# Opening in two halves of the channels, with dummies on TensorE, a joined router and a shorter first gather, in a two-layer diffusion kernel

## What is computed

```python
for layer in range(DEPTH):
    last = layer == DEPTH - 1
    mod_l = (cond_lat @ w_mod[layer] + b_mod[layer])[:, None, :]
    sh1, sc1, gt1, sh2, sc2, gt2 = jnp.split(mod_l, 6, axis=-1)
    ...
    h_l = modulate(rmsnorm(x, g_norm1[layer]), sh1, sc1)
    out_l, out_c = token_mixer(h_l, h_c, w_in[layer], ...)
    x = x + gt1 * out_l
    h_l = modulate(rmsnorm(x, g_norm2[layer]), sh2, sc2)
    y = swiglu(h, ...) if layer % 2 == 0 else moe_swiglu(h, w_router, b_router, w1, w3, w2)
    x = x + gt2 * y
return rmsnorm(x, g_final)

def moe_swiglu(h, w_router, b_router, w1, w3, w2):
    logits = (h @ w_router).astype(jnp.float32) + b_router.astype(jnp.float32)
    top_v, top_i = lax.top_k(logits, TOP_K)
    top_w = jax.nn.softmax(top_v, axis=-1)
    combine = jnp.sum(jax.nn.one_hot(top_i, N_EXPERTS, dtype=jnp.float32) * top_w[..., None], axis=-2)
    for e in range(N_EXPERTS):
        out = out + combine[..., e:e + 1] * swiglu(h, w1[e], w3[e], w2[e])
```

## Time and profile before

| | us |
|---|---|
| median of 3 runs | 1991.55 (1990.99 to 1991.76) |
| profiled execution | 1990.3 |
| its span | 1988.5 |
| PE busy | 1925.8 |
| DVE busy | 1365.7 |
| ACT busy | 991.1 |

### The profile page before, as it was taken

One profiled execution on the slowest core, in us unless ns is written; L12 is line 12 of the kernel. 1 busy time (PEld: TensorE's weight loads), 2 busy tenths in 40 slices (PEclk: granted clock), 3 DMA queues, 4 the chain that ended last, 5 costly groups with the idle time before them and its releaser, 6 DMA issues.

```text
span 1988.5 us, 23322 instructions
## 1 busy us (share of the span) xinstructions
PE 1925.8 (97%) x9008; PEld 1532.1 (77%) x9008; DVE 1365.7 (69%) x1606; ACT 991.1 (50%) x1098; POOL 87.6 (4%) x127
## 2 busy tenths in 40 slices
PE   6999999999899999989999989999999999999997
PEld 3785666667688888868788978888888888888886
DVE  5752444477667646546354558989898988898995
ACT  3423333322522222244434367777777777777774
POOL 0150000010000001001200000000000000000000
PEclk9999999999899999989999979999999999999998
DMA  9322122255256556513234279999998999999980
GB/s 375 127 74 67 61 75 96 85 181 168 94 181 191 180 180 232 193 64 138 85 120 156 96 307 358 356 349 356 349 357 346 358 347 357 347 359 348 358 329 22
DMA packets 72398, 438.67 MB, mean 221 GB/s; under 512 B 9184, under 2 KB 9952, under 8 KB 28000
## 3 DMA queue, kind: packets, MB, share of 16 engines
q1 hardware_dynamic: 60624, 394.18, 52.9%
q0 software_dynamic: 11664, 43.00, 6.8%
HBM read 436.09 MB, written 1.05 MB: 220 GB/s over the span
## 4 chain that ended last, share of the span: by engine, by line
PE 90%; DVE 4%; ACT 3%; issue 1%; DMA 0%; SPq 0%; ACTq 0%; DVEq 0%
PE ps L1630 12%; PE ps L1631 12%; PE ps L1632 12%; PE ps L2020 8%; PE ps L2022 8%; PE ps L2021 7%; PE ps L1865 6%; PE ps L2034 4%; PE ps L2035 4%; PE ps L2038 4%; PE ps L1814 2%; PE ps L1773 2%; DVE elo L1443 1%; PE ps L1664 1%; PE ps L1840 1%
## 5 line engine op out<-in xcount | busy, mean ns | idle before, releaser
L1443 DVE TENSOR_TENSOR elo<-estage,ehi 128x2048 fp32r<-128x2048 f32 x264 | 604.8, 2291 | 74.4 <-ACT ehi L945 67.9
L945 ACT ACTIVATE ehi<-estage 128x2048 fp32r<-128x2048 f32 x264 | 505.4, 1914 | 53.9 <-PE ps L2038 50.4
L1630 PE MATMUL ps<-h_hi,whi 128*128 128x512 f32 (+1 forms) x960 | 369.6, 385 | 16.1 <-DVE h_lo L1098 8.8
L1631 PE MATMUL ps<-h_lo,whi 128*128 128x512 f32 (+1 forms) x960 | 346.8, 361 | 0.0
L1632 PE MATMUL ps<-h_hi,wlo 128*128 128x512 f32 (+1 forms) x960 | 346.6, 361 | 0.0
L2020 PE MATMUL ps<-ehi,xg_hi 128*128 128x512 f32 x704 | 283.9, 403 | 2.1 <-DVE xg_lo L1456 2.1
L2022 PE MATMUL ps<-ehi,xg_lo 128*128 128x512 f32 x704 | 276.3, 392 | 0.0
L2021 PE MATMUL ps<-elo,xg_hi 128*128 128x512 f32 x704 | 275.5, 391 | 0.0
L1058 DVE TENSOR_TENSOR wlo<-stage,whi 128x2048 fp32r<-128x2048 f32 x79 | 182.2, 2306 | 97.0 <-ACT whi L687 96.9
L687 ACT ACTIVATE whi<-stage 128x2048 fp32r<-128x2048 f32 x79 | 150.8, 1909 | 164.6 <-PE ps L1632 163.9
L1630 PEld LDWEIGHTS ps<-h_hi,whi 128*128 128x128 f32 x960 | 183.2, 191 | 57.9 <-issue 19.1
(11 more groups left out here) (224 smaller groups left out, 2331.7 us busy)
## 6 DMA issues: line engine op xcount, KB each, us to landing
estage<-in_moe SPq DMA_DIRECT2D x264, 1024.0 KB, 5.0
stage<-in_split SPq DMA_DIRECT2D x79, 1024.0 KB, 4.9
gw<-in_mods POOLq DMA_DIRECT2D x80, 512.0 KB, 4.0
dw<-in_direct SPq DMA_DIRECT2D x36, 512.0 KB, 3.7
mw_b<-in_mods SPq DMA_DIRECT2D x8, 512.0 KB, 12.7
mw_a<-in_early SPq DMA_DIRECT2D x8, 512.0 KB, 14.2
xT<-in_x SPq DMA_DIRECT2D x1, 2048.0 KB, 7.9
gw<-in_cond_rows SPq DMA_DIRECT2D x1, 1024.0 KB, 5.4
```

Source lines behind the costliest of these rows:

```text
L945: act.activation(ehi[:, w % SPLIT, :], estage[:, w % STAGE, :], ACT.Copy).then_inc(S("e_hi_done"), 1)
L1443: dve.tensor_tensor(elo[:, w % SPLIT, :], estage[:, w % STAGE, :], ehi[:, w % SPLIT, :], ALU.subtract)\
L1630: pe.matmul(out, hi, rhs_hi, start=first, stop=False)
L1631: pe.matmul(out, hi, rhs_lo, start=False, stop=False)
```

## The change

1. **Opening.** x is loaded in four DMAs ahead of everything but the condition; its squares go through DVE's adds, as in the other norms. The shifts and the scales (four groups of 512 columns) all come from PE: each group's 8 rows run in four column tiles of 32 columns (`cond_32`, the condition padded to 32 columns), and a matrix `pick` sums the four tiles while it turns them. Groups 0 and 1 hold shift and scale of channels 0 to 511, groups 2 and 3 of channels 512 to 1023; the norm's first half needs the first two. DVE's start units are gone, the `cond_rows` load and the work on it come behind the norm, and split unit 1 is placed inside the norm.
2. **Norms n1_0, n2_0, n1_1.** The second half (latent tokens) of odd k is scaled by DVE instead of ACT.
3. **Dummies.** `keep_clock` issues 128x128 matmuls whose result nobody reads: 16, 2 and 4 in the opening, 5, 4 and 12 around each later norm, 2 a channel in the router, 6 behind the first gather, 14 ahead of the last scatter.
4. **Out-projection of layer 0.** The last two `merged_lo` stand ahead of the last two modulation units.
5. **Routing.** Small DVE operations are joined over the two token tiles, both logits lie in one bank, the low rows are copied by DVE (ACT did), the first gather multiplies rows by selection the other way round and gives the turned tokens at once, waits are split in halves; exponential, combine and the turned selection move into the first expert.

```diff
@@ modulation rows and turns (PE)
         def early_rows(g):
             pe.wait_ge(S(f"early_in{g}"), 16 * GROUP_UNITS)
-            for k in range(KD):
-                u = GROUP_UNITS * g + k // 2
-                ins = pe.matmul(ps[2 + g][0:2, :], cond_t[:, k, :], mw_a[:, u, k % 2, :], start=(k == 0), stop=(k == KD - 1))
+            quarters = P // TILE_W
+            for i in range(KD // quarters):
+                for q in range(quarters):
+                    k = i * quarters + q
+                    u = GROUP_UNITS * g + k // 2
+                    w = (mw_a, mw_b)[u // (EARLY_UNITS // 2)][:, u % (EARLY_UNITS // 2), k % 2, :]
+                    ins = pe.matmul(ps[2 + g][TILE_W * q:TILE_W * (q + 1), :], cond_32[:, k, :], w, start=(i == 0), stop=(i == KD // quarters - 1))
@@ opening (PE)
-        first_squares()
+        def keep_clock(b, n):
+            for _ in range(n):
+                pe.matmul(ps[b][:, 0:P], ones[:, :], ident[:, :], start=True, stop=True)
+        keep_clock(0, 16)
+        added_squares("n1_0", 0)
+        keep_clock(0, 2)
         early_rows(0)
+        everywhere("n1_0", 0)
         early_rows(1)
         early_turn(0)
-        everywhere("n1_0", 0)
         early_turn(1)
+        early_rows(2)
+        keep_clock(0, 4)
@@ first tile of the in-projection, for each k (PE)
+                    if layer == 0 and j == 0 and k == KD // 4:
+                        early_rows(3)
+                    if layer == 0 and j == 0 and k == KD // 2:
+                        early_turn(2)
+                        early_turn(3)
@@ loads (SP)
+        for k in range(0, KD, 2):
+            sp.dma_start(xT[:, k:k + 2, :], A["x"][:, k:k + 2, :]).then_inc(S(f"x_in{k // 4}"), 16)
+        for u in range(EARLY_UNITS):
+            sp.dma_start(early(u), A["early"][u]).then_inc(S(f"early_in{u // GROUP_UNITS}"), 16)
+            if u == GROUP_UNITS - 1:
+                for t, a in small:
+                    load_small(t, a).then_inc(S("consts"), 16)
+            if u == 2 * GROUP_UNITS - 1:
+                load_split(0)
+        load_split(1)
+        sp.dma_start(gw[:, :, :], A["cond_rows"]).then_inc(S("cond_rows1"), 16)
@@ opening (DVE)
-        cond_rows(1)
-        mod_units("start", 0)
+        for k in range(1, KD - 1):
+            add_square("n1_0", 0, k)
         inverse_root("n1_0", 0)
-        mod_units("start", 1)
...
         split_lo(1)
-        mods(0, EARLY_MODS, FLUSH_TILES[0])
-        dve.wait_ge(S("mod_turned"), EARLY_GROUPS)
-        turned_mods()
-        dve.wait_ge(S("mods"), 4)
-        coefs(0, 0)
+        early_mods(0)
@@ norm (DVE)
+                if tag == "n1_0" and k == KD // 2:
+                    lo(k - 2)
+                    lo(k - 1)
+                    early_mods(1)
...
+                if tag == "n1_0" and k == KD - 2:
+                    split_lo(DENSE_SPLIT)
+                if shared(tag, k):
+                    second_half(k)
@@ norm (ACT)
+                if tag == "n1_0" and k == KD // 2:
+                    hi(k - 1)
+                    row_copies(2)
+                    act.wait_ge(S("norm_coef"), 2)
...
-                for s, at in parts:
+                for s, at in parts[:1] if shared(tag, k) else parts:
...
+                if tag == "n1_0" and k == KD // 2 + 1:
+                    split_hi(DENSE_SPLIT)
@@ merges of layer 0 (DVE)
                 merge(m)
+                if m == NM - 1:
+                    merged_lo(m - BESIDE - 1)
+                    merged_lo(m - BESIDE)
                 after_merge(m)
-                if m > BESIDE:
+                if BESIDE < m < NM - 1:
                     merged_lo(m - BESIDE - 1)
-            merged_lo(KD - 1)
@@ norms n2, n1_1 (PE)
+            keep_clock(7, 5)
             added_squares(f"n2_{layer}", lc)
+            keep_clock(7, 4)
             everywhere(f"n2_{layer}", lc)
+            keep_clock(7, 12)
@@ router (PE)
+            keep_clock(5, 2)
...
+            def first_gather():
+                pe.wait_ge(S("sel"), passed("sel", p) + 2)
+                for f in range(2):
+                    if p == 0 and f == 1:
+                        pe.wait_ge(S("most_ready"), 1)
+                    for n, rows in enumerate((htok_hi, htok_lo)):
+                        if p == 0:
+                            pe.wait_ge(S(("htok_hi", "htok_lo")[n]), 2 * (f + 1))
+                        for k in range(4):
+                            for t in range(2):
+                                ins = pe.matmul(ps[3 + 2 * n + f][:, k * SLOTS:(k + 1) * SLOTS], rows[:, t, (4 * f + k) * P:(4 * f + k + 1) * P], sel[:, t, :],
+                                                start=(t == 0), stop=(t == 1))
+                        ins.then_inc(S(("ga_full", "gt_full")[n]), 1)
...
-            gather(0, 0, 0)
-            gather(0, 0, 1)
+            first_gather()
+            if p == 0:
+                keep_clock(2, 6)
@@ first expert (DVE), tail (PE)
+                    if p == 0 and kind == "w" and cc == 2:
+                        combine()
+                        dve.sem_inc(S("comb"), 1)
...
+        keep_clock(2, 14)
         last_scatter("fn")
```

More of the change, by code:

```diff
@@ L191, in mod_plan @@
     return plan
-MOD_FLUSH = [("start", 1), ("in", 0, NT - 1), ("out", 0, KD - 2), ("upu", 4), ("down", 1, 3)]
+MOD_FLUSH = [("in", 0, NT - 1), ("out", 0, KD - 2), ("upu", 4), ("down", 1, 3)]
 def flush_units(n):
-    tiles = [("start", 0), ("start", 1)] + [key for key, _ in split_stream()]
+    tiles = [key for key, _ in split_stream()]
     upto = tiles.index(MOD_FLUSH[n])
@@ L478, in build @@
     junk = {
-        "start": Region(pool_in_at).take("junk_start", [P, D]),
         "in": Region(br_at + 2 * KB * T * 4).take("junk_in", [P, D]),
@@ L1189, in _ @@
             norm(f"n1_{layer}", 0)
+            if layer == 0:
+                cond_rows(1)
             for j, name in enumerate(TILES):
```

283 lines of the change are left out of this document (164 added, 119 removed).

## The result

| | us, median | runs |
|---|---|---|
| before | 1991.27 (1990.83 to 1991.76) | 4 |
| changed | 1972.41 (1971.67 to 1974.48) | 4 |

The ratio is 0.9908, 95% interval 0.9896 to 0.992: 18.9 us less, where the forecast's terms sum to 21.2. The profiled execution of the changed kernel took 1974.48, the longest of the four; its span is 1972.7, 15.8 less than before's. A second profile of the same kernel has a span of 1970.8 (17.7 less).

A forecast was written before the change was run, and what follows sets the result against it. TensorE (PE) was taken as the bound, busy 1925.8 of 1988.5 us, so only its waits and half clock could give time. Terms 7.0 + 4.4 + 1.0 + 6.5 (routing net) + 2.3 = 21.2 gave median 1970.3, range 1962 to 1982.

The forecast's parts named there:

- Opening, 7.0: Start to end of the first two in-projection tiles: reordered loads and four-tile modulation rows end the pair 7.0 us earlier.
- Out-projection, 4.4: Layer 0's out-projection: with ym_lo first, PE's 2.8 us wait and 1.6 us of half clock go, 4.4 us.
- Norms, 1.0: Norms n2_0 and n1_1: dummies in PE's waits and odd channels' second half on DVE give 1.0 us together.
- Routing, 9.0 before the costs: Routing: full clock, fewer small operations and a shorter gather start the first expert's second unit 9.0 us earlier.
- Given back, 2.3: First expert: table loads moved there cost 1.6 us and combine 0.7, against the routing's gain.
- Tail, 2.3: Tail: dummies bring its one-column records and scatter to full clock, 2.3 us, from 0.9 to 2.9.
- (d): Rival, chance 0.18: gaps refill at the pair's end or in the first expert; 5 us less gain, 1975.
- (e): Rival, chance 0.14: routing's transposes lose the clock, the gather behind them too; routing gives 3 less, 1973.
- (b): Rival, chance 0.08: the opening's four column tiles run one after another, 6.9 us a group; opening gives about 0, 1977.
- (a): Rival, chance 0.12: clock falls in the router; routing and norms give 0, tail 0.5; about 1980.
- (c): Rival, chance 0.08: all dummies at half clock, routing +8; with opening rows at half clock too, opening gives 3; about 1996.

The follow-up runs named there:

- all three edits: Changed kernel with the exponential in ACT's idle time, combine joined over both token tiles, and the first expert's turned selection half a step earlier: 1969.30 us.

## Why the prediction was right, and where not

The time, 1972.4, lies 2.1 us above the forecast 1970.3 and well inside the range. By its own steps:

- **Opening, 7.0.** Measured 2.95 and 5.1 with the change's dummies, 5.8 to 6.8 in the other traces that keep both them and the place of unit 1, 7.1 and 7.6 without dummies in the opening. Without any, the chain came as forecast: first product 31.77 (31.7 to 33.5 said), the fifth channel at 46.1 (45.4 to 47.4), the pair done at 56.5 (53.8 to 57.4), a group in 1.92 us (2). On the changed kernel itself the signs named for it failed: first product 35.49 and 33.96, the fifth h_lo 49.3 and 47.7, the pair at 61.1 and 59.0. The step that failed is one that the prediction put at nothing without a reason: 22 dummies ahead of the first product. In the six traces that have them and the four tiles, the first product starts at 34.0 to 35.5. Two chains are late there, and which of them ends last differs. On PE's side the third group's weights land 1.2 to 2.1 us later, beside the code load above, and the four dummies behind the group take 1.2 to 1.7 (at half clock, partly or all). On the norm's side the two dummies behind the squares stand in the way of the first group, 1.1 us at half clock, and h_lo is ready at 32.5 to 33.9 instead of 31.7; in the second profile this alone sets the start. The 16 at the start end 3.8 and 2.7 us ahead of the squares in the changed kernel's two profiles, and the squares run at half clock there. How much of the loss is the code load and how much the dummies' own time was not separated. The prediction failed too in taking the clock as full up to the pair's end; behind PE's wait of 4.1 us it was at half, and from the fifth channel to the pair's end it is 9.4 to 11.7 us by when it came back.
- **Out-projection, 4.4.** 4.7 in every trace, 4.67 alone on the kernel before.
- **Norms, 1.0.** 1.8 in the two traces of the changed kernel, 1.05 from the dummies on the kernel before; between -0.1 and 1.8 in the others with these dummies and between -0.9 and 0.7 in those without. The term is right in size, and smaller than what moves it.
- **Routing, 9.0 before the costs.** 8.1 to 8.2, but the reasons were mixed. I counted full clock for counts, transposes, gather and the first unit as part of it. The kernel before gains 1.7 with the dummies, so of 8.1 at full clock the shorter chain carries 6.4: logits to mask, three counts ahead of the positions, low copies on DVE, no copy and turn behind the gather. Which of these carries how much was not separated. On the new chain the dummies are worth nothing: without them it gains 8.5 (7.4 to 8.7 in the three other traces without them), as the clock comes back by itself at about the counts.
- **Given back, 2.3.** It was 4.1. The mechanism was right and the sum too small: the table loads cost 1.5 (1.6 said), combine about 1.0 (0.7 said), and some 0.3 come with the turned selection that was moved with them, which the prediction left out. 1.4 are left with all three edits and unexplained; with its routing 8 us shorter, the expert starts with fewer units split ahead, which was only argued and not tried.
- **Tail, 2.3.** 2.35 and 2.13; -0.6 without dummies. 1.7 on the kernel before, 1.6 to 2.5 in the other traces with unbroken dummies, 0.4 and 0.9 where PE stood idle amid them.

By the medians 18.9 us came of 21.2, by the two profiles 15.8 and 17.7. Norms and out gave 1.1 more than forecast, the routing 0.9 less. How near the median lies to the forecast is in part luck, since two executions of the same kernel differ by 2.1 us in the opening alone. The better end of the range, 1962, is a slip: even the sum of all upper bounds, 28.3 us, gives 1963.3.

Of the rivals, (d), gaps refill, came partly true: in the opening and the first expert together 5.8 us of the forecast were missing in the first profile, 3.8 in the second. (e), the transposes lose the clock, did not on the changed kernel: the 12 at 1157.82 run at 0.126 us each, so the rule of the Trainium skill (Part 4 of "TensorE: Matmul & The Clock Gate") that was weighed there does not hold for these. On the kernel before with the dummies, though, 16 of them ran at 0.23 each, at half clock, behind a wait and the counts. (b) had the right price for a group of rows run serially, 6.9 (7.05), and the wrong one for the kernel: it said 1977 and the run gave 1987.4. Its first group took 9.3 us, half of them at half clock, so the second was done at 35.4 and not at 28, the third at 44.2, and the first product came at 45.1; the fourth group then pushed the second half by the 5 us that (b) has. (a) and (c) rested on dummies at half clock in the router; they ran at full in each trace that had them. But (c)'s price for the opening with its rows at half clock, 3, is what the first profile gave.

## What to carry to other kernels

Work out for each stage what PE waits for at full clock before you pay for the clock: in the routing raising it from 0.61 to 0.94 bought 1.7 of 30 us, since PE then waited for copies and small operations of the other engines, while in the tail, where PE's own matmuls were most of the chain, 14 dummies bought 1 to 3. Put dummies only where they end before the result that PE waits for; every one that stands ahead of a ready operand costs its own time, twice as much at half clock. Look in the DMA view, too, where the instruction queue's packets lie with them and without. And what is moved out of an idle stretch has to be paid where it lands: two table loads and eleven small operations took back 2.5 us, and the first of them fitted into an idle gap of ACT that nobody had used. A kernel with no dummies in the opening and the three edits of the first expert would be the next to try; it was not run.

## What the runs showed of the hardware

- Four column tiles of 32 run nearly fully at once with plain fp32: 16 records of 512 columns in 1.92 us, against 7.05 in one tile, 3.7 times. The Trainium skill ("TensorE: Matmul & The Clock Gate", Part 3, Measured speedup vs the span model) has 2.38 for three tiles; here four gave more than that per tile.
- Executions of one and the same kernel lie 1.0 to 6.6 us apart here (1970.9 to 1977.4 without dummies, 1984.3 to 1989.3 for the kernel before with ym_lo first). Of the latter the slow ones have the lower mean granted clock (0.980 beside 0.982 or 0.983), and in its profiled execution the routing had full clock for 10 us in its middle and was 2.4 us shorter. A stage that no edit touched gained 1.5 us in two traces, by a stretch of 3.4 us at half clock that was missing. So a stage's gain of under 2 us needs more than one profile.
- In the trace without dummies the clock came back from half to full at 1152.8, at the end of 16 fp32 transposes (1149.7 to 1153.0) behind the router's 6.99 us of small matmuls, and stayed full through the counts and 12 transposes more.
- A 16 KB packet of the instruction queue, 0.95 us, at 25.5 to 26.8 went with weights that landed 0.9 to 2.1 us later than where it came later (29.3 to 30.1, against 28.05 to 28.4, over eleven traces). More matmuls ahead moved it forward. That it is the cause was not tried.
